# Expert output summed in PSUM, tokens gathered from the residual, and a third buffer for down matrices

## The reference

```python
hn = rmsnorm(h, norm_ffn)                     # h: the residual after the mixer, 256 x 1024
g_idx = argmax(hn @ w_router_group)           # one of 4 groups
top_v, top_i = top_k(e_sel, 2)                # two of its 8 experts
gates = g_w * softmax(top_v)
# for each expert e, over the tokens routed to it:
#   (silu(x @ w_gate[e]) * (x @ w_up[e])) @ w_down[e], times the gate, added to the token's row
h = h + out
h = rmsnorm(h, final_norm)                    # then block 2: rmsnorm(h, norm1_2) ...
```

## Time and profile before

| | |
|---|---|
| median of 3 runs (lowest to highest) | 958.61 us (957.39 to 959.03) |
| span of the profiled execution | 956.0 us |
| busy: PE, VectorE (DVE), ScalarE (ACT), POOL | 785.3, 473.7, 321.4, 94.3 us |
| moved by DMA | 286.67 MB, mean 300 GB/s |

### The profile page before, as it was taken

The page is one execution under the profiler, slowest core; times in us unless marked ns, Lnnn a source line. Parts: engine busy times, 40 slices in busy tenths (PEclk is TensorE's granted clock), DMA queues, the critical chain, the costliest instruction groups (busy, mean ns, idle before and its releaser), DMA issues.

```text
span 956.0 us, 15768 instructions
## 1 busy us (share of the span) xinstructions
PE 785.3 (82%) x6548; PEld 599.3 (63%) x6548; DVE 473.7 (50%) x834; ACT 321.4 (34%) x527; POOL 94.3 (10%) x114
## 2 busy tenths in 40 slices
PE   6999999999766674756837567368999999999997
PEld 5989999777535342332423335135988888888885
DVE  5855948556323131211313123034868776766766
ACT  6764346733000000000000000002597554444444
POOL 1029664300000000000000000000000000000000
PEclk9999999999979687786877778799999999999999
DMA  9994244578999999999999999999975456555101
GB/s 318 285 339 177 93 172 176 197 284 345 415 429 427 427 426 428 426 427 428 430 428 429 428 429 429 428 428 383 367 246 178 149 191 206 181 176 176 45 1 45
DMA packets 72279, 286.67 MB, mean 300 GB/s; under 512 B 11611, under 2 KB 38433, under 8 KB 59681
## 3 DMA queue, kind: packets, MB, share of 16 engines
q1 hardware_dynamic: 71620, 284.81, 75.7%
q10 hardware_dynamic: 604, 1.10, 0.3%
HBM read 284.85 MB, written 1.05 MB: 299 GB/s over the span
## 4 chain that ended last, share of the span: by engine, by line
PE 55%; DMA 32%; issue 4%; POOL 3%; DVE 3%; ACT 2%; SPq 0%; POOLq 0%; DVEq 0%; ACTq 0%
DMA down_a<-in_w_down_dram 22%; PE bank L644 12%; PE bank L593 10%; PE bank L609 9%; PE bank L2268 5%; PE bank L606 4%; DMA pair_d<-in_w_up_dram 4%; PE bank L621 4%; PE bank L2249 3%; DMA down_b<-in_w_down_dram 3%; DMA ring<-in_w_in_dram 3%; PE bank L2301 1%; PE bank L2215 1%; PE bank L2223 1%; PE bank L2080 1%
## 5 line engine op out<-in xcount | busy, mean ns | idle before, releaser
L573 DVE TENSOR_TENSOR w_lo<-ring,w_hi 128x1024 fp32r<-128x1024 f32 x135 | 173.6, 1286 | 104.2 <-ACT w_hi L563 103.8
L563 ACT ACTIVATE w_hi<-ring 128x1024 fp32r<-128x1024 f32 x136 | 144.3, 1061 | 178.0 <-PE bank L609 64.0
L1754 DVE COPY y_e<-bank 32x256 f32<-32x256 f32 x64 | 27.2, 424 | 235.8 <-PE bank L2268 235.4
L593 PE MATMUL bank<-act_p,w_hi 128*128 128x256 f32 x736 | 137.2, 288 | 2.7 <-issue 1.8
L609 PE MATMUL bank<-act_p,w_hi 128*128 128x512 f32 x344 | 119.1, 397 | 0.0
L593 PEld LDWEIGHTS bank<-act_p,w_hi 128*128 128x128 f32 x736 | 114.9, 192 | 5.4 <-issue 3.5
L1196 ACT ACTIVATE y_e<-bank 32x256 f32<-32x256 f32 x64 | 23.9, 373 | 280.2 <-PE bank L2268 279.8
L593 PE MATMUL bank<-act_p,w_lo 128*128 128x256 f32 x368 | 104.0, 283 | 0.0
L2268 PE MATMUL bank<-down_a,h_t 128*32 128x256 f32 x512 | 45.7, 518 | 63.0 <-DMA down_a<-in_w_down_dram 50.0
L644 PE MATMUL bank<-w_hi,act_q 128*128 128x512 f32 x288 | 90.5, 395 | 1.5 <-issue 1.0
L606 PE MATMUL bank<-act_p,w_lo 128*128 128x256 f32 x344 | 89.4, 280 | 0.0
(11 more groups left out here) (409 smaller groups left out, 1064.4 us busy)
## 6 DMA issues: line engine op xcount, KB each, us to landing
ring<-in_w_up_dram SPq DMA_DIRECT2D x24, 2048.0 KB, 34.2
ring<-in_w_gate_dram SPq DMA_DIRECT2D x23, 2048.0 KB, 29.6
down_a<-in_w_down_dram SPq DMA_DIRECT2D x16, 2048.0 KB, 25.6
down_b<-in_w_down_dram SPq DMA_DIRECT2D x15, 2048.0 KB, 25.6
ring<-in_w_in_dram SPq DMA_DIRECT2D x14, 2048.0 KB, 16.9
ring<-in_w_ffn_in_dram SPq DMA_DIRECT2D x22, 1024.0 KB, 7.6
pair_d<-in_w_gate_dram SPq DMA_DIRECT2D x8, 2048.0 KB, 30.0
pair_d<-in_w_up_dram SPq DMA_DIRECT2D x8, 2048.0 KB, 34.5
```

The costliest lines, as they stand in the source:

```text
L563: nc.scalar.activation(parts(w_hi, g, view), view, ACT.Copy).then_inc(split_hi, 1)
L573: engine.tensor_tensor(parts(w_lo, g, view), view, h, ALU.subtract).then_inc(split_lo, 1)
L593: mm = nc.tensor.matmul(dst, parts(wt, g, grans[g][1])[:, k, :], a[:, x_part, k, :], start=(k == 0 and i == 0), stop=(k == KC - 1 and i == 2))
L1754: ins = nc.vector.tensor_copy(y_e[CAP * e:CAP * (e + 1), 256 * j:256 * (j + 1)], bank[2][CAP * j:CAP * (j + 1), 0:256])
```

## The change

- **Down matrices.** A third buffer `down_c` is laid over mixer tiles. SP loads expert 2's down matrix into it, behind `load_down(0, 0)` and a wait for `ssd_ss` 4 (the last use of those mixer tiles). Group 0 uses the buffers a, b, c, a for its experts 0 to 3; later groups use b, a, b, a.
- **fgain** now lies in `down_c`. SP loads it after the first unit of block 2 and no longer ahead of expert 4's gate. As it shares memory with `lpad`, POOL clears `lpad`'s first columns only after `res_moe` 2.
- **Tokens.** `tok` and ScalarE's two scaling passes go. `gather` and `gather_first` read `res` itself, one feature in eight (`by_feature`), and the one-hot matrices carry 1/rms. For group 0's first gather VectorE multiplies the membership by 1/rms. The two squares go to `y_e`, so VectorE's first copy of the logits waits for `ss_act` 2.
- **Gather.** One `onehot` and one `x_t` buffer. Each half of a gather goes to bank 7: half 0 before down product 2, half 1 behind it and behind VectorE's eviction of half 0.
- **Sum.** All groups accumulate in banks 1, 3, 5, 6 (`add_group`); VectorE adds to `res` once, after the last group.

The core of the diff:

```diff
+    down_c = sb("down_c", [P, UNIT], where=ph)
+    fgain = down_c[:, 0:D]
     y_e = sb("y_e", [P, D], where=ph)
...
+    landed_down = [*(sem(f"landed_down{n}") for n in range(2)), landed_apart]
...
+    DOWN = (down_a, down_b, down_c)
+    MOE_BANK = (1, 3, 5, 6)
+    XT_BANK = 7
+    def down_at(k, e):
+        if isinstance(k, int) and k == 0:
+            return ((0, 1), (1, 1), (2, 2), (0, 2))[e]
+        return ((1, 2 * k), (0, 2 * k + 1), (1, 2 * k + 1), (0, 2 * k + 2))[e]
...
             sp.wait_ge(ye_raw, used)
-            load_down(i, e_down)
+            load_down(1 - i % 2, e_down)
...
                 load_down(0, 0)
+                sp.wait_ge(ssd_ss, 4)
+                load_down(2, 2)
...
         load_down(1, 1)
-        sp.dma_start(fgain[:, :], w["final_norm"].partition_broadcast(P)).then_inc(ld_fgain, 16)
...
-            sp.wait_ge(ye_raw, i)
-            load_down(i - 1, i + 1)
-        sp.wait_ge(ye_raw, 4)
-        load_down(3, 5)
+            sp.wait_ge(ye_raw, i if i < 3 else 4)
+            load_down((i - 1) % 2, i + 2)
...
+            if u == UA:
+                sp.dma_start(fgain, w["final_norm"].partition_broadcast(P)).then_inc(ld_fgain, 16)
...
-        link_pool(pool, nc.gpsimd.memset(lpad[:, :, 0:3], 0.0))
...
         pool.wait_ge(res_moe, 2)
+        nc.gpsimd.memset(lpad[:, :, 0:3], 0.0).then_inc(const_ready, 1)
...
-        for b in range(TB):
-            ins = nc.scalar.activation(by_chunk(tok[:, b, :], True), by_feature(res[:, b, :], True), ACT.Copy,
-                                       scale=sm[:, 4 + b:5 + b])
-        ins.then_inc(nrm_act, 1)
...
+        dve.wait_ge(rstd_ready, 2)
+        link_dve(dve, nc.vector.tensor_tensor(r8[:, 9, :, 1], rt[:, 4, :, 0], sm[:, 4:6], ALU.mult))
         dve.wait_ge(rank_raw, 1)
...
             for b in range(TB):
-                ins = place(b, 0, onehot[:, s, b, :], False)
+                place(b, 0, onehot[:, 0, b, :], sm[:, 4 + b:5 + b])
+                ins = place(b, 1, gtmp[:, b, :], sm[:, 4 + b:5 + b])
             ins.then_inc(built, 1)
...
+            nc.vector.tensor_tensor(onehot[:, 0, :, :], onehot[:, 0, :, :], gtmp, ALU.add).then_inc(built, 1)
...
-        def add_moe(k):
-            for q in range(4):
-                b, half = divmod(q, 2)
-                v = res[:, b, half * 512:(half + 1) * 512]
-                dve.wait_ge(moe_raw, 4 * k + q + 1)
-                nc.vector.tensor_tensor(v, v, bank[M_BANK[q]][:, :], ALU.add).then_inc(moe_added, 1)
...
+        def tokens(b, c):
+            return by_feature(res[:, b, :], True)[:, :, c]
+
+        def gather(k, half):
+            for c in range(4):
+                for b in range(TB):
+                    mm = nc.tensor.matmul(bank[XT_BANK][:, c * P:(c + 1) * P], tokens(b, 4 * half + c),
+                                          onehot[:, 0, b, :], start=(b == 0), stop=(b == TB - 1))
+            mm.then_inc(xt_raw, 1)
...
+        def add_group(k, first, last):
+            pe.wait_ge(ye_act, 4 * k + 4)
+            pe.wait_ge(ye_dve, 4 * k + 4)
+            pe.wait_ge(gmat_kept, k + 1)
+            if last:
+                pe.wait_ge(xt_kept, 2 * k + 6)
             for at, (b, half) in enumerate(BY_HALF):
+                mm = nc.tensor.matmul(bank[MOE_BANK[at]][:, :], gmat[:, b * P:(b + 1) * P],
+                                      y_e[:, half * 512:(half + 1) * 512], start=first, stop=last)
...
-            down_pe(4 * k + 1, 1, 2 * k + 1, False)
-            gather(k + 1, 1 - s)
-            down_pe(4 * k + 2, 2, 2 * k + 2, False)
+            down_pe(k, 1)
+            pe.wait_ge(built, 4 * k + 6)
+            pe.wait_ge(gmat_kept, k + 1)
+            gather(k + 1, 0)
+            down_pe(k, 2)
+            pe.wait_ge(xt_kept, 2 * k + 5)
+            gather(k + 1, 1)
 
         pe.wait_ge(member, 2)
-        pe.wait_ge(nrm_act, 2)
```

More of the change, by code:

```diff
@@ L292, in build @@
     landed_pair = [sem(f"landed_pair{n}") for n in range(2)]
-    landed_down = [sem(f"landed_down{n}") for n in range(2)]
+    landed_down = [*(sem(f"landed_down{n}") for n in range(2)), landed_apart]
     const_ready = sem("const_ready")
@@ L1703, in build_group, with keep_xt @@
                 dve.wait_ge(routed, 1)
+            dve.wait_ge(built, 4 * k + 2)
             for b in range(TB):
-                place(b, 0, gated[:, b, :], True)
-                ins = place(b, 1, gtmp[:, b, :], True)
+                place(b, 0, gated[:, b, :], pos[:, b, 2:3])
+                ins = place(b, 1, gtmp[:, b, :], pos[:, b, 3:4])
             ins.then_inc(built, 1)
-            dve.wait_ge(built, 3 if before is None else 4 * before + 3)
-            nc.vector.tensor_tensor(gated[:, :, :], gated[:, :, :], gtmp[:, :, :], ALU.add)
+            dve.wait_ge(built, 4 * k + 3)
+            nc.vector.tensor_tensor(gated, gated, gtmp, ALU.add)
             nc.vector.tensor_scalar(pos[:, :, 0:2], pos[:, :, 0:2], -float(P), None, ALU.add).then_inc(built, 1)
-        def keep_xt(k, s):
-            for half in range(2):
-                dve.wait_ge(xt_raw, 2 * k + (half + 3))
-                nc.vector.tensor_tensor(
-                    x_t[:, s, 4 * half:4 * half + 4, :],
-                    bank[5 + half][:, :].rearrange("p (c j) -> p c j", c=4),
-                    bcast(g_ffn[:, 4 * half:4 * half + 4].unsqueeze(2), [P, 4, P]), ALU.mult).then_inc(xt_kept, 1)
+        def keep_xt(k, half):
+            dve.wait_ge(xt_raw, 2 * k + (half + 3))
+            nc.vector.tensor_tensor(
+                x_t[:, 4 * half:4 * half + 4, :], bank[XT_BANK][:, :].rearrange("p (c j) -> p c j", c=4),
+                bcast(g_ffn[:, 4 * half:4 * half + 4].unsqueeze(2), [P, 4, P]), ALU.mult).then_inc(xt_kept, 1)
         def keep_first(half):
@@ L1731, in keep_rest @@
                 nc.vector.tensor_tensor(
[L1732 removed]
+                    x_t[:, 4 * half:4 * half + 4, CAP:P],
                     bank[5 + half][:, 0:4 * n].rearrange("p (c j) -> p c j", c=4),
                     bcast(g_ffn[:, 4 * half:4 * half + 4].unsqueeze(2), [P, 4, n]), ALU.mult).then_inc(xt_kept, 1)
[L1736 to L1737 removed]
+        build_group(0)
         keep_rest()
@@ L1780, in group_dve @@
                         keep_right(4 * before + 3, 3)
-                        add_moe(before)
                     dve.wait_ge(gmat_raw, k + 1)
@@ L2205, in _ @@
         keep_running(2)
-        def gather(k, s):
-            pe.wait_ge(built, 4 * k + 2)
-            for half in range(2):
-                for c in range(4):
-                    for b in range(TB):
-                        o = (4 * half + c) * P
-                        mm = nc.tensor.matmul(bank[5 + half][:, c * P:(c + 1) * P], tok[:, b, o:o + P],
-                                              onehot[:, s, b, :], start=(b == 0), stop=(b == TB - 1))
-                mm.then_inc(xt_raw, 1)
+        def tokens(b, c):
[6 more added lines that the diff above has]
+            mm.then_inc(xt_raw, 1)
         def gather_first(o, n, banks, which):
@@ L2278, in close_last @@
             pe.wait_ge(gmat_kept, k + 1)
-            pe.wait_ge(moe_added, 4 * k + 1)
-            pe.wait_ge(xt_kept, 2 * k + 6)
+            if last:
+                pe.wait_ge(xt_kept, 2 * k + 6)
             for at, (b, half) in enumerate(BY_HALF):
-                nc.tensor.matmul(bank[LAST_MOE_BANK[at]][:, :], gmat[:, b * P:(b + 1) * P],
-                                 y_e[:, half * 512:(half + 1) * 512], start=True, stop=True).then_inc(moe_raw, 1)
+                mm = nc.tensor.matmul(bank[MOE_BANK[at]][:, :], gmat[:, b * P:(b + 1) * P],
+                                      y_e[:, half * 512:(half + 1) * 512], start=first, stop=last)
+                if last:
+                    mm.then_inc(moe_raw, 1)
+        def close_last(k):
+            down_pe(k, 3, ring[:, LAST_DOWN, :])
+            add_group(k, False, True)
             for c in range(KC):
                 if c % 4 == 0:
-                    pe.wait_ge(moe_added, 4 * k + (3 + c // 2))
+                    pe.wait_ge(moe_added, 2 + c // 2)
                 for b in range(TB):
@@ L2292, in close_group, with group_pe @@
         def close_group(k):
-            down_pe(4 * k + 3, 3, 2 * k + 2, False)
-            pe.wait_ge(ye_act, 4 * k + 4)
-            pe.wait_ge(ye_dve, 4 * k + 4)
-            pe.wait_ge(gmat_kept, k + 1)
-            for q in range(4):
-                b, half = divmod(q, 2)
-                pe.wait_ge(moe_added, 4 * k + max(1, q))
-                nc.tensor.matmul(bank[M_BANK[q]][:, :], gmat[:, b * P:(b + 1) * P],
-                                 y_e[:, half * 512:(half + 1) * 512], start=True, stop=True).then_inc(moe_raw, 1)
-        def group_pe(k, before, s):
+            down_pe(k, 3)
+            add_group(k, isinstance(k, int) and k == 0, False)
+        def group_pe(k, before):
             if before is not None:
                 pe.wait_ge(xt_kept, 2 * k + 4)
-                gate_up_pe(k, s, 0)
+                gate_up_pe(k, 0)
```

135 lines of the change are left out of this document (63 added, 72 removed).

## The result

| | before | after |
|---|---|---|
| median (lowest to highest) of 4 runs | 958.27 us (957.39 to 959.03) | 968.44 us (966.95 to 969.12) |
| span of the profiled execution | 956.0 us | 967.4 us |
| busy: PE, VectorE, ScalarE, POOL | 785.3, 473.7, 321.4, 94.3 us | 819.2, 459.0, 317.4, 94.1 us |

The ratio is 1.0102, with an interval of 95% from 1.0090 to 1.0114: 10.2 us slower, where 4.9 us faster was forecast. The work of VectorE and ScalarE shrank by 15 and 4 us, as the diff says. PE's grew by 34 us, with 6548 instructions in either kernel.

A forecast was written before the change was run, and what follows sets the result against it. The experts' weight stream, DMA full at 428 GB/s from 246 to 638 us, was taken as the bound. The moved down matrix gave -4.9, all else 0: 958.61 - 4.9 = 953.7 us, range 951.0 to 957.5.

The forecast's parts named there:

- A transfer leaves the full stretch: Expert 2's 2.097 MB down load moves from the full DMA stream into idle mixer time, issued about 177.1: -4.9 us.
- The share in the hole: DMA share at 186 to 201 us in the mixer, 0.39 before, expected near 0.72 with the early down load.
- The stream is not starved: After expert 5's pair, queued loads last until 283.6; the fourth down product is done by 264.9, so no cost.
- fgain, PSUM sum, copies, placing, each 0: Moved fgain load, adds leaving VectorE, dropped ScalarE copies, group 0's changed placing: each taken to change the time by 0.
- The strided operand, 0: PE's gather loads from `res` with a stride of 8 elements keep their 112 ns pitch: 0, upper bound 3.2 us.
- The bound that I drew from it, +50 ns: At most 50 ns more on each of the 64 gather loads ahead of the stream: 3.2 us.
- The slow rival: Strided read doubles the gather loads' pitch: +7.2 for 64 loads, +2.5 in the last group, -4.9: 963.4 us; chance 0.06.
- At the end, both strands move by 4.9: PE's closing products and the second block's first unit both hang on DMA landings, so both come 4.9 us earlier.
- PE's landing strand: Sign of a wrong forecast: the second block starts on PE's products after the last half pair, not on its unit.
- a pair issued after 244: Sign of a wrong forecast: SP issues expert 5's pair, which starts the stream, after 244 instead of at 242.4.
- No gain because the return loop sets the pace: Rival: down fetches wait for products two experts earlier, so the early load saves nothing: 958.6 us; chance 0.06.
- more gain from the holes: Rival: shorter routing work closes DMA holes at 230 to 234 and 244 to 246: up to 3.2 more, 950.5; chance 0.06.

The follow-up runs named there:

- plain_late: plain_gather with expert 2's down matrix loaded behind the first group's products instead of in the mixer: 957.90 us, ratio 0.9996.
- plain_gather: The changed kernel with every gather reading 128 adjacent columns of the residual instead of one in eight: 953.16 us, ratio 0.9945.
- before_strided: The kernel before with `tok` kept in natural order and the gathers reading it one column in eight: 975.59 us, ratio 1.0175.

## Why the prediction was wrong

**A transfer leaves the full stretch, -4.9: right.** plain_late less plain_gather is 4.9, and 4.3 to 5.3 in their traces. The loads left at 178.43 and 178.81 (177.30 and 177.68 in plain_gather) for the 177.1 of the text, and nothing queued behind them was late: 190.06 is that execution's 188.41. The share in the hole was 0.78 and 0.71 for the 0.72 that was worked out.

**The stream is not starved: right.** In plain_gather the fourth down product runs from 264.03 to 265.94, for the 264.9 that its end was put at, and the share stays at 1.01.

**fgain, PSUM sum, copies, placing, each 0: right as a sum, and only as one.** plain_late is the kernel before within 0.2%, and its pair of expert 5 leaves at 242.65 for 242.44. The parts were not tried one by one, so a gain in one and a loss in another stay possible.

**The strided operand, 0: this step failed.** The row that I chose was the nearest in tile and step, and it was of another operation. PE's transposes do load `res` with that step, in 190 ns against 140, and start 16 within 2.0 us. But a transpose's load isn't a matmul's. The kernel before had a row that says so: its gather loads, plain, take 192 ns, where a plain transpose load takes 140. What is 50 ns on the one is 142 on the other (334), and the pitch, which stays in the transposes, doubles from 112 to 240. The bound that I drew from it, +50 ns, was no bound. The second piece of evidence was misread too: ScalarE's copy of 2.05 us walks its source in natural order and its target with a step of 128 elements, so it isn't the read that is strided. (In before_strided, where the target's step is gone, the same copy takes 1.14 us.) It spoke of a step's cost all the same, and so did the rule of the Trainium skill (SBUF — State Buffer, section Door 1: The DMA port swizzle) that I let the transposes outvote.

**The slow rival: right in mechanism, short in size.** It gave +7.2 for 64 loads (measured +8.0), +2.5 in the last group (+2.7 in the profile, 3.5 in the medians) and -4.9: +4.8, and 10.2 came. The missing term is the clock: toward the end of each gather, in which the array mostly waited for its weights, the clock fell to half, and the products behind it ran on that, 4.3 us more on two gate-ups that the diff doesn't touch. The rest is under 1 us. (The 2.4 us of low clock at the router and in the mixer are in the profile's 11.4, not in this sum; whether the median has them isn't known.)

**At the end, both strands move by 4.9: right without the step, wrong with it.** In plain_gather the unit lands at 661.15 (660.8 in the text). In the changed kernel PE's landing strand took over, which the text names as a sign that the forecast is wrong, beside the other sign, a pair issued after 244.

**The other rivals.** No gain because the return loop sets the pace, and more gain from the holes: neither was seen. The share stayed at 1.01 (plain_gather) and the pair didn't leave early.

The chances were wrong as well. Everything but one term rested on rows of the same operation, and that one term, multiplied by 64 on the path, got 0.06 on the strength of a row of another.

## What to carry to other kernels

A price is taken from a row of the same operation as well as the same operand; if a plain row of both is at hand (192 against 140 here), compare them first. The fp32 weight load of a matmul wanted at least two neighbours in each 16 bytes here; where the layout can't give that, let another engine turn the data once, in work that it does anyway. Slow loads on a path ahead of a full transfer stream can be paid twice: by their own time, and by the clock of what follows. A count of loads is taken from the trace's records, not from the products in the text of the kernel.

## What the runs showed of the hardware

- An fp32 weight load of 128x128 with a step of 16 or 32 bytes takes 330 to 336 ns in place of 192, and such loads follow each other every 240 ns in place of 112. With 8 bytes it takes 197.
- A transpose's load pays less, and at every step: 190 ns with 32 bytes, 212 with 16, 209 with 8, against 140 with none. With 32 bytes its pitch stays (16 start within 2.0 us, plain within 1.9).
- ScalarE's copy of 128x1024 takes 2.05 us with a step of 128 elements in its target and 1.14 without (before_strided).
- VectorE's 128x512 add of fp32 takes 1.03 to 1.10 us in place of 0.69 with a step of 8 as with one of 128 elements.
- A stream in which the gate and up matrices come in pieces of 16, 8, 4 and 2 KB ran at 428, 424, 415 and 400 GB/s.
- PE at "100% busy" in a gather was an array that mostly waited for weights: in each kernel with a step of 16 or 32 bytes in the first group the clock fell to half toward the end of both of its gathers, and neither time when fillers ran in between.
